# Modulation columns moved from the tensor engine to the vector engine, and six tiles of a projection run on the input ahead of its norm

## What is computed

```python
mod = silu(c) @ w_mod + b_mod          # six parts of 1024: shift, scale, gate, twice
x   = rmsnorm(h, final_g)              # end of the first model
xn  = rmsnorm(x, norm1_w) * (1 + scale) + shift
proj = xn @ w_in                       # 1536 columns "qkv_b", and the rest
qkv_b = silu(causal_conv4(proj_qkv_b)) # per channel, over the sequence
beta, g = sigmoid(b_b), -exp(a_log) * softplus(a_b + dt_bias)   # 8 columns of proj
...
```

## Time and profile before

| what | value |
|---|---|
| runs | 1329.17, 1329.63, 1338.44 us |
| median | 1329.63 us |
| the profiled execution | 1336.81 us |
| its span in the profile | 1335.0 us |
| TensorE busy | 1299.7 us, 9416 matmuls |
| VectorE busy | 809.0 us |
| ScalarE busy | 612.6 us |
| GpSimd busy | 55.1 us |

### The profile page before, as it was taken

How to read it: one execution, slowest core, us unless ns; L and a number is a source line. 1 busy time by engine, 2 the same in 40 slices (tenths; PEclk the granted TensorE clock), 3 DMA queues, 4 the chain that set the end, 5 groups by cost and what they waited for, 6 DMA issues and landing times. The chain is left out here.

```text
span 1335.0 us, 24633 instructions
## 1 busy us (share of the span) xinstructions
PE 1299.7 (97%) x9416; PEld 1133.9 (85%) x9416; DVE 809.0 (61%) x1461; ACT 612.6 (46%) x1047; POOL 55.1 (4%) x97
## 2 busy tenths in 40 slices
PE   6999999999999999999999999999999999999996
PEld 5999999999999998789999989989999974444444
DVE  6477567588776677467888757858644752222214
ACT  4545545445444555455444446656533441111112
POOL 0100020000000000000000000000000000000000
PEclk9999999999999999999999999999988989999999
DMA  9775455566667644235676776432144659999994
GB/s 375 173 240 187 143 168 190 182 220 224 210 226 237 206 158 135 82 104 190 234 237 230 251 247 220 159 112 78 64 158 173 213 212 401 384 417 418 418 418 167
DMA packets 83287, 295.78 MB, mean 222 GB/s; under 512 B 11062, under 2 KB 12086, under 8 KB 83056
## 3 DMA queue, kind: packets, MB, share of 16 engines
q1 hardware_dynamic: 70992, 257.39, 53.4%
q0 software_dynamic: 12192, 36.95, 9.1%
HBM read 287.76 MB, written 11.53 MB: 224 GB/s over the span
## 5 line engine op out<-in xcount | busy, mean ns | idle before, releaser
L2122 DVE TENSOR_TENSOR ring_low<-ring,w_hi 128x1024 fp32r<-128x1024 f32 x292 | 355.4, 1223 | 196.1 <-ACT w_hi L1640 195.4
L851 PE MATMUL bank<-hn_hi,w_hi 128*128 128x272 f32 (+1 forms) x1416 | 413.9, 292 | 4.6 <-DVE hn_low L2143 3.9
L855 PE MATMUL bank<-hn_hi,ring_low 128*128 128x272 f32 (+1 forms) x1416 | 407.2, 288 | 0.0
L854 PE MATMUL bank<-hn_low,w_hi 128*128 128x272 f32 (+1 forms) x1416 | 406.4, 287 | 0.0
L1640 ACT ACTIVATE w_hi<-ring 128x1024 fp32r<-128x1024 f32 x292 | 302.3, 1051 | 119.5 <-PE bank L851 107.1
L851 PEld LDWEIGHTS bank<-hn_hi,w_hi 128*128 128x128 f32 x1416 | 270.3, 191 | 9.0 <-DVE hn_low L2143 4.9
L855 PEld LDWEIGHTS bank<-hn_hi,ring_low 128*128 128x128 f32 x1416 | 270.6, 191 | 0.0
L854 PEld LDWEIGHTS bank<-hn_low,w_hi 128*128 128x128 f32 x1416 | 270.4, 191 | 0.3
L851 PE MATMUL bank<-arena_r,w_hi 128*128 128x256 f32 (+1 forms) x816 | 234.0, 287 | 2.9 <-DVE arena L2370 2.2
L855 PE MATMUL bank<-arena_r,ring_low 128*128 128x256 f32 (+1 forms) x816 | 232.4, 285 | 0.0
L854 PE MATMUL bank<-arena_r,w_hi 128*128 128x256 f32 (+1 forms) x816 | 231.9, 284 | 0.0
(11 more groups left out here) (463 smaller groups left out, 1614.5 us busy)
## 6 DMA issues: line engine op xcount, KB each, us to landing
ring<-weights SPq DMA_DIRECT2D x396, 512.0 KB, 4.2
mod_part<-mod_rows POOLq DMA_DIRECT2D x40, 512.0 KB, 4.7
w_late<-weights SPq DMA_DIRECT2D x28, 512.0 KB
tab<-weights SPq DMA_DIRECT2D x28, 512.0 KB
arena<-weights SPq DMA_DIRECT2D x24, 512.0 KB
tab<-tables SPq DMA_DIRECT2D x1, 2858.0 KB, 17.4
arena<-weights POOLq DMA_DIRECT2D x5, 512.0 KB, 5.5
skew<-arena POOLq DMA_DIRECT2D x1, 2048.0 KB, 47.9
```

The lines of the kernel that those rows point to most:

```text
L851: begun = mm(dst[:, 0:cols], wh, high(k), start=k == 0, stop=False)
L854: mm(dst[:, 0:cols], wh, low(k), start=False, stop=False)
L855: last = mm(dst[:, 0:cols], wl, high(k), start=False, stop=k == K - 1)
L2122: tt_(ring_lo[:, slot, :], ring[:, slot, :], w_hi[:, n % SPLITS, :], ALU.subtract).then_inc(S("w_lo_ready"), 1)
```

## The change

- The eight modulation units leave the stream, with `mod_sum`, `mod_store`, `mod_join` and `mod_add`. VectorE makes all 48 tiles: two more in the retention heads 2 and 3, and seven instead of one under "wo0" (k = 1 to 7). GpSimd loads six rows instead of four ahead of the sixteen transfers of the attention bias.
- During "down1" the residual is also split as s * x into `first_hi` (ScalarE) and `first_lo` (VectorE), without the norm; their columns 256 and 257 hold the shift.
- t0 to t5 of "qkvb" run on these 258 columns, straight behind "down1"; the row sums of the squares come inside t0, ahead of its k-block 4. VectorE evacuates these six tiles (`first_tile`): it multiplies by the reciprocal root and copies the shift's column, and ScalarE adds that column as a bias afterwards. t6 to t11 run on the normalised input as before.
- VectorE does t0's evacuation and the decay columns ahead of the eight norm tiles, t1 to t4 among them and t5 behind. ScalarE splits a unit behind every second norm tile. The chain of beta and g stands behind the six tiles, and the sums of g behind t9.

```diff
-MOD_TILES = LATE_MOD * 4
+MOD_TILES = MODS * DT
+RET_MODS = 2 * RH - 3
+UNNORMED = 6
+WIDE = 258
...
-            for n in range(RH):
+            for n in range(RET_MODS + 1):
...
-            pe.wait_ge(S("c_silu"), 1)
-            mod_two(LATE_MOD, both_norms)
...
-            with_decay_inputs(hb, hb_lo, SEQ, split_ready("n1"))
+            hu, hu_lo = (lambda k: first_hi[:, k, 0:WIDE]), (lambda k: first_lo[:, k, 0:WIDE])
+
+            def first_ready(k):
+                split_ready("n1u")(k)
+                if k == DT // 2:
+                    both_norms()
+
+            with_decay_inputs(hu, hu_lo, WIDE, first_ready)
             for t in range(1, 12):
-                dense(DT, hb, hb_lo, SEQ)
+                if t < UNNORMED:
+                    dense(DT, hu, hu_lo, WIDE)
+                else:
+                    dense(DT, hb, hb_lo, SEQ, split_ready("n1") if t == UNNORMED else None)
...
-                if t == 6:
+                if t == 9:
                     pe.wait_ge(S("g_ready"), 1)
...
+                fn(first_hi[:, k, 0:SEQ], h[:, k, XC], ACT.Copy, scale=mod[:, DT + k:DT + k + 1])\
+                    .then_inc(S("x_hi_ready"), 1)
...
-            mod_store(10)
-            mod_store(11)
+            highs(at["qkvb"])
...
+                if k % 2:
+                    highs(at["qkvb"] + k // 2 + 1)
...
+            for t in range(UNNORMED):
+                highs(at["qkvb"] + t)
+                wait_stored(act, at["qkvb"] + t)
+                fn(raw_b[:, t, CONV - 1:], raw_b[:, t, CONV - 1:], ACT.Identity, bias=col_bias[:, t:t + 1])\
+                    .then_inc(S("x_hi_ready"), 1)
+            tile[0] = at["qkvb"] + UNNORMED
...
+                if hh > 1:
+                    mod_tile()
...
-                          lambda k: hn_lo[:, k, :], "ffn0", (3,))
+                          lambda k: hn_lo[:, k, :], "ffn0", range(1, DT))
...
-            add_tiles(at["down1"], SEQ, lambda k: h[:, k, XC], "n1", 7)
+            shift_in = mod[:, 0:DT].unsqueeze(2).to_broadcast([P, DT, WIDE - SEQ])
+            link(nc.vector.tensor_copy(first_hi[:, :, SEQ:WIDE], shift_in))
+            tt_(first_lo[:, :, SEQ:WIDE], shift_in, first_hi[:, :, SEQ:WIDE], ALU.subtract)
+            add_and_split(at["down1"], SEQ, lambda k: h[:, k, XC], "n1", None, lambda k: first_hi[:, k, 0:SEQ],
+                          lambda k: first_lo[:, k, 0:SEQ], "n1u", range(7))
...
+            def first_tile(t):
+                src, free = take(at["qkvb"] + t)
+                tt_(raw_b[:, t, CONV - 1:], src[:, 0:SEQ], rstd[:, 0:SEQ], ALU.mult)
+                nc.vector.tensor_copy(col_bias[:, t:t + 1], src[:, SEQ:SEQ + 1]).then_inc(free, 1)
+
+            first_tile(0)
...
-                        lambda k: mod[:, k:k + 1])
-            mod_add(10)
-            mod_add(11)
...
+                        lambda k: mod[:, k:k + 1], lambda k: first_tile(k // 2) if k and k % 2 == 0 else None)
+            for t in range(DT // 2 + 1, UNNORMED):
+                first_tile(t)
```

More of the change, by code:

```diff
@@ L519, in wait_stored, with tiles @@
             eng.wait_ge(evacuated[n % BANKS], freed(n))
-        at, tile_unit, mod_units = {}, [], set()
+        at, tile_unit = {}, []
         blocks = 0
-        def tiles(name, count, each, of_mod=False):
+        def tiles(name, count, each):
             nonlocal blocks
@@ L606, in build @@
         assert blocks == EXPERTS_FIRST * UB
-        dense_units = [u for u in range(EXPERTS_FIRST) if u not in mod_units]
+        dense_units = list(range(EXPERTS_FIRST))
         split_no = {u: n for n, u in enumerate(dense_units)}
@@ L775, in _ @@
                                    bass.AP(skew.tensor, a * flat + off, [[511, P], [1, n]])).then_inc(S("bias_loaded"), 16)
-            for n in range(RH, MOD_TILES):
+            for n in range(RET_MODS + 1, MOD_TILES):
                 pool.wait_ge(mod_used, n)
@@ L965, in turn_tiles @@
                     last.then_inc(tile_done, 1)
[L967 to L993, removed]
-                    last = mm(bank[t % BANKS][:, q:q + 1], mod_part[:, g % 2, q * P:(q + 1) * P], C("quad", 0, 1),
-                              start=True, stop=True)
-                last.then_inc(tile_done, 1)
-            def mod_two(g, sums):
-                mod_sum(g)
-                sums()
-                mod_sum(g + 1)
-                mod_join(g)
-                mod_join(g + 1)
             pe.wait_ge(S("ones_set"), 1)
@@ L1493, in gather @@
                 if ready:
-                    pe.wait_ge(S("x_split"), all_split + ready)
+                    pe.wait_ge(S("x_split"), all_lows + ready)
                 for k in range(2 * part, 2 * part + 2):
@@ L1654, in x_high @@
                     fn(hi(k), src(k), ACT.Copy).then_inc(S("x_hi_ready"), 1)
-            def mod_store(g):
-                act.wait_ge(mod_used, MOD_TILES)
-                t = mod_summed[g]
-                highs(t)
-                act.wait_ge(tile_done, done(t))
-                fn(mod_part[:, g % 2, :], bank[t % BANKS][:, :], ACT.Copy).then_inc(evacuated[t % BANKS], 1)
             def root(name, cols, width, total=bank[7], bias=None):
@@ L1727, in _ @@
                     fn(wba_hi[:, :], V("wba", 0, DT * 8), ACT.Copy).then_inc(S("wba_hi_ready"), 1)
-                    fn(small[:, 0:DT], V("c", 0, DT), ACT.Silu).then_inc(S("c_silu"), 1)
                 if hh == 1:
@@ L1895, in raw_tile @@
                 fn(raw_b[:, t, CONV - 1:], src[:, 0:SEQ], ACT.Copy).then_inc(free, 1)
-            for t in range(3):
-                raw_tile(t)
-            highs(at["qkvb"] + 3)
             act.wait_ge(S("ba_split"), 2)
@@ L1910, in conv_silu @@
                     fn(cb[:, t, :], cb[:, t, :], ACT.Silu).then_inc(S("conv_silu"), 1)
-            for t in range(3, 12):
+            for t in range(UNNORMED, 12):
                 raw_tile(t)
@@ L2278, in _ @@
             dve.wait_ge(S("skew_written"), 16)
-            def add_tiles(first, cols, dst, name, mods):
-                for k in range(DT):
-                    if k > 1:
-                        add_squares(name, k - 1, cols)
-                    src, free = take(first + k)
-                    tt_(dst(k), dst(k), src[:, 0:cols], ALU.add).then_inc(free, 1)
-                    if k < mods:
-                        mod_tile()
             def add_squares(name, k, cols):
@@ L2301, in low @@
                     dve.wait_ge(S("x_hi_ready"), split_first[split] + k + 1)
[L2302 removed]
+                    g = mod[:, DT + k:DT + k + 1] if gain is None else V(gain, k)
+                    stt(lo(k), x(k), g, hi(k), ALU.mult, ALU.subtract).then_inc(S("x_split"), 1)
                 for k in range(DT):
```

49 lines of the change are left out of this document (18 added, 31 removed).

## The result

The changed kernel takes 1340.26 us (median of 18 runs, 1337.96 to 1346.01); the kernel before, over the runs beside it, 1330.21. The ratio is 1.0073, 95% interval 1.0063 to 1.0082: about 10 us slower. The prediction was 1337.3 us, range 1322 to 1345. The profiled execution of the changed kernel took 1341.24 us, span 1339.4.

A forecast was written before the change was run, and what follows sets the result against it. TensorE, busy 97% of the span, was taken as the bound. -6.3 (t0) + 2.8 + 7.2 + 2.4 (stalls) + 1.7 (clock), less 0.1 rounding, gave +7.7: 1337.3 us, range 1322 to 1345.

The forecast's parts named there:

- Gain at the end of t0: First qkvb tile: modulation columns and joins leave TensorE, so t0 ends at 802.4 instead of 808.76, 6.3 us gained.
- Stall in t6: qkvb's first tile from normalised input: TensorE waits 2.8 us for the last norm low, due at 822.45.
- Stall at u9: Before t9: TensorE waits 7.2 us for u9's low part, behind ScalarE's table loads and eight conv products.
- my walk: VectorE's and ScalarE's work through qkvb, priced in program order; by it t11 ends at 849.3 instead of 841.57.
- Stall at u10: Before t10: u10's low part stands behind VectorE's wait for the sums of g; 2.4 us.
- The clock: Halved clock behind the 7.2 us stall costs 1.7 us; 0 for the other two, bounds 0 and 1.7.
- my two rows: Clock evidence: 3.94 us idle at kernel start left the clock at 0.50; 1.46 before 893.33 left it at 1.00.
- The base: Kernel before: median 1329.63 us, to which +7.7 us was added, giving 1337.3.
- The modulation rows in wo0: Six more VectorE reductions under wo0: last row up to 2 us late but covered; cost 0, bounds 0 and 3.
- rival C: Modulation rows land late in wo0, counting from a landing of about 5.5 us: 1352 us; chance 0.11.
- Rival B: In qkvb the supply keeps up, no wait for u9 and u10, TensorE keeps its gain: 1323.3 us; chance 0.17.
- Rival D: Part of the shift is given back later (1.46 us wait at 893), or u9's stall halves: 1331 to 1333; chance 0.12.

The follow-up runs named there:

- Experiment 2: Changed kernel with only ScalarE's high parts of u4 to u7 written ahead of the norm tiles: 1336.68 us, ratio 1.0034 to the kernel before.
- Experiment 1: Changed kernel, order mended: u4 to u7 high parts before norm tiles, u9 before table loads and decay chain, u10 to u12 before sums of g: 1330.2 us (0.9986).
- Experiment 3: Changed kernel with only u9's high part before table loads, its low part before the decay chain, u10 to u12 before sums of g: 1335.11 us (1.0023).
- experiment 7: Kernel of experiment 5 with TensorE's 16 l2 sums in one piece behind qka's last tile: 1331.03 us (0.9986).
- the tenth experiment: Kernel of experiment 9 with all 16 l2 sums in va, four ahead of each of its first four k-blocks: 1325.56 us (0.9953).
- experiment 9: Kernel of the eighth with l2 sums split between qka's last tile and va, first two qka tiles stored ahead of the decay matrix: 1331.0 us (0.9993).
- experiment 5: Kernel of experiment 1 with sums of g copied between conv products, u16 and u17 split before the decay matrix, later qka units earlier: 1337.24 us (1.004).
- the eighth: Kernel of experiment 7 with ScalarE's conv activations one tile later and u13 one place earlier: 1329.09 us (0.9973).
- the fourth: One part of the change alone: all 48 modulation rows on VectorE, first tiles from the normalised input as before: 1332.29 us (1.0001).

## Why the prediction was right, and where it was off

- **Gain at the end of t0.** Predicted 6.3, measured 6.53.
- **Stall in t6**, from a pitch of 4.4 us per unit: the pitch was 4.33 (816.40 to 820.74 on VectorE) and the stall 2.02 where I had 2.8. The last norm low began at 822.28, where I had it there at 822.45, and t0 had begun 0.85 later than I took (0.51 of it from the start of the kernel on: the wait at 16.14 ends at 16.65 here). Experiment 2 shows that the mutual waiting was its cause.
- **Stall at u9.** Predicted 7.2, measured 5.90, with the table loads, the eight products and u9's low part in the order named; that low part began at 835.16, where my walk gives 834.6. TensorE came to it later than in my walk, having just lost 1.7 us to the clock, and what it loses before a wait shortens the wait: the two together are 7.6. Experiments 1 and 3 remove the stall by order alone.
- **Stall at u10.** Predicted 2.4, measured 2.55.
- **The clock: the term that was mis-sized.** I charged 1.7 us once, for the longest stall, and took 0 for those of 2.8 and 2.4, as lying nearer to the 1.46 us that had cost nothing. It fell behind all three, and cost 1.7, 2.0 and 3.0. The first 1.7 vanished in the wait for u9, as I had written: from t1 to u9's low part neither VectorE nor ScalarE waits for TensorE, so t9 begins when they are ready, at 836.53 where my walk has 835.7. What was wrong is the 0 for the stall at u10, with 1.7 as its bound: it was 3.0. From t0's start to the end of t11 my walk has 849.3 - 793.9 = 55.4 us and the profile 853.24 - 794.76 = 58.5, 3.1 more, of which t10 and t11 make 2.75: 8.45 us (844.79 to 853.24) in place of 5.7.
- **A row that I did not read.** The kernel before has a wait of a length between my two rows; its timeline, and the window behind:

```profile
1050.23 0.39 PE L875 MATMUL bank<-arena_r,w_hi 128*128 128x256 f32 x1 [2.10 <-DVE ring_low L2122]
...
1050.00:1056.00 6.00, 5.77 (x35) 0.72 0.77 311
```

  That is 6 x 0.28 = 1.7 us lost behind 2.10. By this row the stall at u10 costs 1.7, and the forecast is 1339.0. But the same wait stands in all thirteen profiles, 2.09 to 2.11 us long, and in three (experiments 1, 2 and 7) the clock stayed at 1.00 behind it. Experiment 1:

```profile
1047.16 0.39 PE L863 MATMUL bank<-arena_r,w_hi 128*128 128x256 f32 x1 [2.10 <-DVE ring_low L2078]
...
1047.00:1053.00 6.00, 5.84 (x48) 1.00 0.77 307
```

  What such a wait costs in one execution could not be had from its length.
- **The base.** I forecast +7.7 us and +10.05 came. The other 0.6 between 1337.3 and 1340.26 is the kernel before, whose median is 1330.21 over 18 runs and was 1329.63 over my three. I also wrote that a measurement can hardly tell 13.3 us from no change; the interval here is 1.3 us to each side.
- **The modulation rows in wo0** cost next to nothing on the path, but with no margin left. VectorE waited for a row there five times, up to 2.19 us, and three times in later stages, up to 2.45:

```profile
256.32 1.29 DVE L2139 CUSTOM_DVE_ANT_0 mod_part<-mod_part,arena,vec 128x1024 f32<-128x1024 f32 x1 [2.19 <-DMA mod_part<-mod_rows]
...
767.78 1.29 DVE L2139 CUSTOM_DVE_ANT_0 mod_part<-mod_part,arena,vec 128x1024 f32<-128x1024 f32 x1 [2.45 <-DMA mod_part<-mod_rows]
```

  The 2 us of lateness that I had worked out were right, and rival C, 1352 us, did not come: the landing was 4.6 in the median, 4.8 for the rows of wo0. But 5.5 as the landing from which it counts was wrong by my own terms: the slack from 254.8 to 257.49, over six tiles, is gone at 1.28 + 0.4 + 4.8 us per row. And so it was. The last low part of the norm began at 257.54 and TensorE's weight load waited 0.15 us for it:

```profile
258.09 0.19 PEld L863 LDWEIGHTS bank<-hn_hi,w_hi 128*128 128x128 f32 x1 [0.15 <-DVE hn_low L2245]
```

  TensorE's distance to the kernel before grew there by 0.2 us, from 0.50 at 208 to 0.71 at 511.
- **Rival B**, that the supply keeps up, 1323.3 us, was false for this order and true for a better one: the tenth experiment is at 1325.56. What I had not seen is that mending the order in qkvb does not suffice. Three more steps behind it had been in time only because TensorE came later: the sums of g, u16, and the squares.
- **Rival D**, that the 1.46 us at 893 would shrink, was wrong: 1.46 or 1.47 in every kernel. It is a dependence between engines that moves along with TensorE.

## What to carry to other kernels

When TensorE's stream gets shorter ahead of a stage and nothing leaves the engines that feed it, walk those engines' program order through every later step until the slack of the old schedule is larger than the gain; here there were six such places of over 1.5 us, and two of about 1, in some 40 us, and each mended one showed the next. Let an engine that writes weights for TensorE do so before it waits for anything else, and put no long chain (table loads, a small sum from TensorE) ahead of the next unit. Give each wait of 2 us or more a second term for the clock behind it, as a range: here 0 to 3.0 us, most often 1.7, and more where one-column matmuls followed.

## What was not expected of the hardware

- What a wait costs in clock does not follow its length. Losses read from the windows: 1.7 us behind 2.02, 3.0 behind 2.55, 2.0 behind 5.90 (the changed kernel), 1.7 behind 2.55 and 2.9 behind 5.39 (experiment 2), 1.7 behind 3.06 (experiment 1), 1.7 or nothing behind 2.10 (above). It was 5.2 behind 1.91 (experiment 9) and 8.5 behind 3.00 (experiment 5), where one-column matmuls stood between the others; that these were the reason is not shown. The rule of the Trainium skill ("TensorE: Matmul & The Clock Gate", section "What's actually happening") that recent activity releases a throttled clock fits all of these, but does not tell them apart. Read as the forecast weighed it, every wait here can cost more than its length, and by that the result would have been 1.7 us later than mine; it was 3.
- The clock also fell without any wait: behind 3.5 us of one-column matmuls (experiments 7 and 8), and in the profiled execution of before from 985 to 1020 us, in the middle of dense work (0.76 in the mean; 0.90 in experiment 1, 1.00 in the changed kernel). Why it did there, nothing here shows.
- The same 1.46 us wait at 893 us left the clock at 1.00 in the kernels before and after, but behind it the mean was 0.72 over 892 to 898 in the eighth and over 896 to 902 in the fourth. The eighth's runs spread from 1325.99 to 1334.64 us, those of the tenth, 6 of them, from 1324.83 to 1328.06.
